# Linear recurrence on one core: where VectorE issues the low parts of the output gate's two panels, against the sixth level of the recurrence

## The reference

```
proj = rmsnorm(h) @ w_in                    # hq, hf, hi, hgo, hz, nq, kcm, ..., ngate, nz
f    = lb + (1 - lb) * sigmoid(hf);  k = (1 - lb) * sigmoid(-hf)
S_t  = diag(f_t) S_{t-1} + k_t v_t^T;  o_t = S_t^T q_t            # v = hi, q = hq
y_hg = rmsnorm(o) * sigmoid(hgo) * silu(hz)
y_nsa = (gated sum of compressed, selected and window attention) * silu(nz)
h = h + concat(y_hg, y_nsa) @ w_out
```

## Time and profile before

| | |
|---|---|
| median of 3 runs | 971.55 us (971.46 to 971.69) |
| profiled execution | 971.99 us |
| its span, first to last instruction | 970.0 us |
| mean granted TensorE clock | 0.999 |
| TensorE (matmuls) busy | 953.6 us, 98% |
| VectorE busy | 754.3 us, 78% |
| ScalarE busy | 615.6 us, 63% |

### The profile page before, as it was taken

One profiled execution on the slowest core, in us unless ns is written; L12 is line 12 of the kernel. 1 busy time (PEld: TensorE's weight loads), 2 busy tenths in 40 slices (PEclk: granted clock), 3 DMA queues, 4 the chain that ended last, 5 costly groups with the idle time before them and its releaser, 6 DMA issues.

```text
span 970.0 us, 18775 instructions
## 1 busy us (share of the span) xinstructions
PE 953.6 (98%) x7618; PEld 875.2 (90%) x7618; DVE 754.3 (78%) x1132; ACT 615.6 (63%) x914; POOL 19.7 (2%) x33
## 2 busy tenths in 40 slices
PE   6999999999999999999999999999999999999997
PEld 6998989999989889999999999999998988888886
DVE  7967876797678777998788877778878598777685
ACT  5744885676447856787477556557657566555554
POOL 2000200000002000000000000000000000000000
PEclk9999999999999999999999999999999999999999
DMA  9666422465664233745546656557283446655541
GB/s 304 197 181 219 139 88 87 137 214 183 173 218 139 66 110 115 244 156 188 179 133 215 218 175 200 187 174 222 93 271 110 141 135 219 203 181 176 191 152 44
DMA packets 143869, 164.33 MB, mean 169 GB/s; under 512 B 6686, under 2 KB 130216, under 8 KB 143800
## 3 DMA queue, kind: packets, MB, share of 16 engines
q1 hardware_dynamic: 142408, 161.90, 51.9%
q0 software_dynamic: 928, 0.52, 0.4%
q10 hardware_dynamic: 464, 0.93, 0.3%
HBM read 161.89 MB, written 1.05 MB: 168 GB/s over the span
## 4 chain that ended last, share of the span: by engine, by line
PE 87%; DVE 5%; ACT 4%; DMA 2%; issue 1%; SPq 0%; DVEq 0%; ACTq 0%
PE ps L479 19%; PE ps L480 18%; PE ps L481 18%; PE ps L1259 14%; PE ps L1257 7%; DMA panels<-in_w_in 2%; DVE panels_low L2026 2%; ACT panels_high L1393 2%; PE ps L497 1%; PE ps L692 1%; PE ps L717 1%; PE ps L788 1%; PE ps L1299 1%; DVE squares L1989 1%; PE ps L703 1%
## 5 line engine op out<-in xcount | busy, mean ns | idle before, releaser
L2026 DVE TENSOR_TENSOR panels_low<-panels,panels_high 128x2048 fp32r<-128x2048 f32 (+1 forms) x145 | 327.5, 2261 | 63.2 <-ACT panels_high L1393 62.6
L1393 ACT CAST panels_high<-panels 128x2048 fp32r<-128x2048 f32 (+1 forms) x145 | 273.4, 1887 | 85.7 <-PE ps L481 63.2
L479 PE MATMUL ps<-input_parts,panels_low 128*128 128x256 f32 x832 | 240.2, 289 | 0.2 <-DVE panels_low L2026 0.2
L480 PE MATMUL ps<-input_parts,panels_high 128*128 128x256 f32 x832 | 235.2, 283 | 0.0
L481 PE MATMUL ps<-input_parts,panels_high 128*128 128x256 f32 x832 | 235.1, 283 | 0.0
L1259 PE MATMUL ps<-input_parts,panels_high 128*128 128x512 f32 x608 | 214.0, 396 | 0.0
L1257 PE MATMUL ps<-input_parts,panels_low 128*128 128x256 f32 x608 | 170.6, 281 | 0.7 <-DVE panels_low L2026 0.7
L479 PEld LDWEIGHTS ps<-input_parts,panels_low 128*128 128x128 f32 x832 | 159.2, 191 | 2.4 <-issue 1.7
L480 PEld LDWEIGHTS ps<-input_parts,panels_high 128*128 128x128 f32 x832 | 159.3, 191 | 0.7 <-issue 0.5
L481 PEld LDWEIGHTS ps<-input_parts,panels_high 128*128 128x128 f32 x832 | 159.3, 191 | 0.0
L1259 PEld LDWEIGHTS ps<-input_parts,panels_high 128*128 128x128 f32 x608 | 114.1, 188 | 26.4
(11 more groups left out here) (342 smaller groups left out, 1626.6 us busy)
## 6 DMA issues: line engine op xcount, KB each, us to landing
panels<-in_ffn_up SPq DMA_DIRECT2D x44, 1024.0 KB, 5.0
panels<-in_w_in SPq DMA_DIRECT2D x29, 1024.0 KB, 5.8
panels<-in_ffn_down SPq DMA_DIRECT2D x22, 1024.0 KB, 4.9
panels<-in_mix_w_in SPq DMA_DIRECT2D x20, 1024.0 KB, 5.7
panels<-in_w_out SPq DMA_DIRECT2D x8, 1024.0 KB, 5.3
panels<-in_w_pg SPq DMA_DIRECT2D x8, 1024.0 KB, 5.1
panels<-in_mix_w_out SPq DMA_DIRECT2D x8, 1024.0 KB, 5.2
panels<-in_w_in SPq DMA_DIRECT2D x6, 512.0 KB, 5.7
```

What stands on the lines that cost most here:

```text
L479: pe.matmul(dst, w[1], x[0], start=start, stop=False if not kw else True, **kw)
L480: pe.matmul(dst, w[0], x[1], start=False, stop=False if not kw else True, **kw)
L1393: nc.scalar.copy(high_slots[slot][:, 0:size], raw[n % SLOTS][:, 0:size]).then_inc(high_ready, 1)
L2026: V.tensor_tensor(low_slots[slot][:, 0:size], raw[n % SLOTS][:, 0:size], high_slots[slot][:, 0:size].bitcast(F32), ALU.subtract).then_inc( ...
```

## The change

Its description: VectorE takes the sixth level's copies and scalings ahead of the low part of the output gate's second panel.

In VectorE's program the call at the head of "gates" goes, and one with the cap of hgo1 is put at the end of "hidden". The call at the head of "hidden" (L2358), with the same cap, stays.

```diff
                     elif kind == "gates":
-                        split_low(place)
                         for n in range(NT):
                             drained(dve, f"vv{n}_{l}")
                         link(V.tensor_scalar(GT[:, :], GT[:, :], 1.0, None, ALU.add))
...
                         V.tensor_copy(HIDV[:, :].rearrange("p (g r c) -> p g r c", g=2, r=4),
                                       HID[:, 32:64].rearrange("p (g c) -> p g c", g=2).unsqueeze(2)
                                       .to_broadcast([P, 2, 4, 16])).then_inc(hidden_ready, 1)
+                        split_low(place, SPLIT_NO[("hgo1", l)] + 1)
                     elif kind == "cmp_kv":
```

## The result

| | before | after |
|---|---|---|
| median | 971.60 us (971.46 to 971.69, 4 runs) | 983.39 us (982.93 to 983.72, 4 runs) |
| profiled execution | 971.99 us, span 970.0 | 982.93 us, span 981.1 |
| mean granted TensorE clock | 0.999 | 0.992 |

The ratio is 1.012, with a 95% interval from 1.0108 to 1.0132: slower by 11.8 us. That lies in the third case of the prediction, both falls (981.1 to 984.0), which had a chance of 0.25; the forecast itself was 980.6.

What follows compares the result with a forecast made beforehand. TensorE, busy 98% of the span, was taken to bound the kernel. Order +7.27 us and one clock fall +1.8 gave +9.1, so 980.6 us on the median of 971.55; range 978.3 to 983.3.

Steps and rivals of the forecast that it cites:

- the third case of the prediction, both falls: TensorE's clock falls in the stalls of both layers: 981.1 to 984.0 us, chance 0.25.
- the order's part of the size: Second half of hgo0 later on TensorE in layers 0 and 1, without the clock: sum +7.27 us.
- the likeliest case: One fall of TensorE's clock for the two stalls: 980.6 us, own range 979.7 to 981.6, chance 0.42.
- What the change does: VectorE's call at the head of "hidden" issues both low parts behind the sixth level; the added call finds nothing left.
- The case with only hgo1's: Only hgo1's low part moves, hgo0's stays at 84.23, L788's stall goes: 969.8 us, chance 0.05.
- Start of the sixth level, 87.67: VectorE, layer 0: sixth level's copies start 0.50 us behind its matmuls' start, bounds 0.35 and 0.60.
- its 2.78: VectorE, layer 0: the sixth level's copies and scalings take 2.78 us, next operation at 90.45.
- the low part's 2.29: VectorE, layer 0: hgo0's low part takes 2.29 us behind the sixth level, ending at 92.74.
- the start at 92.79: TensorE, layer 0: first half of hgo0 starts at 92.79 instead of 88.26, held 4.53 us.
- The second half of hgo0, +3.59 and +3.68.: TensorE: second half of hgo0 starts 3.59 us later in layer 0 and 3.68 in layer 1.
- What is queued behind costs nothing.: hgo1's low part, hidden, seventh level, panel loads and rope terms come later, within TensorE's shift or slack: no cost.
- the fifth case, late loads: hz1 lands over 2.4 us late and holds ScalarE: another 1 to 3 us per layer, 981 to 986, chance 0.03.

Runs made afterwards that it cites:

- the filled run: 30 matmuls that nobody needs added on TensorE ahead of its wait for hgo0's low part, against the changed kernel; 979.24 us.
- the run with the short stall: hgo0's low part issued between the halves of the sixth level instead of behind both, against the changed kernel; 979.94 us.

## Why the prediction was right, and which term was off

The direction, the place and the order's part of the size came out as reckoned; the likeliest case was not the one that came, and the median stands at the upper edge of the range.

1. **What the change does** was read right: both low parts move, the added call finds nothing left. The group of two L2026 at 90.37 shows it. The case with only hgo1's would have been 969.8, and measures 969.58.
2. **Start of the sixth level, 87.67; its 2.78; the low part's 2.29; the start at 92.79.** Measured 87.52 (with TensorE's own matmuls 0.14 earlier), 2.85 and 92.80. The idle time reads 4.51 for the 4.37 reckoned. The first half of hgo0 starts 5.77 us behind the sixth level's matmuls, 4.68 more than before (88.26 - 87.17 = 1.09), where 4.53 was reckoned.
3. **The second half of hgo0, +3.59 and +3.68.** With the clock held up it is +3.58 in layer 0, and the filled run is 7.6 above before, for a sum of 7.27. The near hit in layer 0 is in part luck: in the filled run the first half of hgo0 is 4.59 later against the sixth level (reckoned 4.53) and its matmuls take 3.06 (reckoned 2.98), while the seventh level takes 1.07 (reckoned 1.22).
4. **What is queued behind costs nothing.** Holds: VectorE did the seventh level from 98.6 to 100.6, TensorE's waits show nothing for it, and moving hgo1's low part past hidden changes nothing that can be told. ScalarE took the high part of hz1 at 103.00, with no idle time before it, so the fifth case, late loads, didn't come.
5. **The clock: "I take one fall for the two stalls: +1.8."** This is the term that failed. Both stalls had their fall in the profiled execution, and each cost 2.1 by the filled run (4.15 for the two), inside the bounds of 1.15 to 2.6 but above the middle. So the term is 2.35 too small: 2.1 for the second fall, 0.3 for the price. That is most of the 2.8 us by which the forecast is low (and the median 0.1 above the range); 7.27 + 4.15 is 11.4, and the 0.4 that is left to 11.8 is in the order (7.6 for 7.27). The way the price was reckoned holds: behind the stall 21 matmuls start in 4.62 us (92.80 to 97.42), 0.22 apart, where they stand 0.12 apart at full speed, and 0.44 of 4.6 us is 2.0.

The choice of one fall rested on one sample, the fall 3.1 us after the kernel's last matmul. In the changed kernel it came after 2.4 us, and in the run with the short stall 4.5 us after the last matmul ahead of the stall, with 1.5 us of new work in between. One delay, read once, was taken for a threshold, and 4.37 us for a stall close to it.

Each of the five stalls of 4.5 us that were profiled (two in the changed kernel, two with hgo1 behind hidden, one with the change in layer 0 alone) was followed by a stretch at 0.50. The Trainium skill (TensorE: Matmul & The Clock Gate, "HAM oscillation") says that behind a long enough wait between bursts of matmuls the next burst starts cold, every time. With these stalls this case's traces agree.

## What to carry over

A call that issues "whatever is due" can hold more than one thing. Before it is moved, list what it issues in the order of the pointer, and check each item against its own consumer: here one low part could move and gained 2.0 us, the other one had its consumer waiting for it and cost 13.8, together 11.8. And where a change makes TensorE stand still for some microseconds (2.9 and more did it here, not each time), price the stall and the slow stretch behind it as two terms, and give each stall its own slow stretch; here the second term was over half of the first.

## What was not expected of the hardware

- The clock can fall after TensorE has gone back to work: at 93.2 with the stream resumed at 91.71, and at 94.0 with the stream resumed at 92.85. Who reads the clock of the stall alone sees 1.00 in both.
- Idle times of 2.9 to 3.0 us cost the clock in three of four cases, and the same idle time of 2.92 us did and didn't within one execution. Idle times of 0.5 to 0.8 us never did.
- Useless matmuls in a stall are worth 4.15 us here (30 per layer) and 3.9 us in the short stall (20 per layer), while the first half of hgo0 starts within 0.1 us of the same distance behind the sixth level.
